# Token rows instead of feature rows for the values, gates and outputs of two recurrent phases

## The reference, cut to what matters

```python
# gated linear attention ("gla"): 4 heads, keys 128, values 256
S_t = diag(a_t) S_{t-1} + k_t^T v_t ;  o_t = q_t S_t      # a_t: forget gate
o_gla = rms_norm(o_gla, gla_out_norm) * silu(rg)          # norm over the 256 values of a head
# HGRN2 ("hg"): 16 heads, keys 128, values 128, the same recurrence with
# q = silu(.), forget = sigmoid(.), k = 1 - forget
o_hg = rms_norm_2(o_hg, hg_out_norm) * gate               # norm over the 128 values of a head
```

## Time and profile before

| | |
|---|---|
| median of 3 runs | 3389.58 us (3389.53 to 3390.03) |
| the profiled execution | 3386.4 us, its span 3384.6 us, granted clock 0.997 |
| PE matmul busy | 98% |
| DVE, ACT, POOL busy | 68%, 51%, 11% |
| DMA | 592 MB, 175 GB/s, queue 1 busy 56.1% |

### The profile page before, as it was taken

The page is one execution under the profiler, slowest core; times in us unless marked ns, Lnnn a source line. Parts: engine busy times, 40 slices in busy tenths (PEclk is TensorE's granted clock), DMA queues, the critical chain, the costliest instruction groups (busy, mean ns, idle before and its releaser), DMA issues.

```text
span 3384.6 us, 56343 instructions
## 1 busy us (share of the span) xinstructions
PE 3317.2 (98%) x18614; PEld 2866.3 (85%) x18614; DVE 2285.4 (68%) x3419; ACT 1714.9 (51%) x2500; POOL 379.8 (11%) x422
## 2 busy tenths in 40 slices
PE   8999999999999998999999999999999999999999
PEld 7888888887788877888888888888888888888888
DVE  6666666676656866665665677787666668656566
ACT  5444444454544655444444456774444444555554
POOL 1000000010022311000000001220242422100000
PEclk9999999999999999999999999999999999999999
DMA  7566566664544554666666655556544445555555
GB/s 227 186 199 187 185 192 186 188 190 144 160 147 148 193 155 138 187 190 187 187 191 187 185 181 176 189 178 188 162 149 149 149 149 164 184 162 180 169 168 166
DMA packets 236026, 592.48 MB, mean 175 GB/s; under 512 B 18832, under 2 KB 113296, under 8 KB 235808
## 3 DMA queue, kind: packets, MB, share of 16 engines
q1 hardware_dynamic: 234784, 587.12, 56.1%
q10 hardware_dynamic: 1152, 4.19, 0.3%
HBM read 589.14 MB, written 2.10 MB: 175 GB/s over the span
## 4 chain that ended last, share of the span: by engine, by line
PE 52%; issue 10%; DVE 3%; ACT 1%; POOL 1%; ACTq 0%; POOLq 0%
PE bank L495 31%; PE bank L494 8%; PE bank L497 8%; PE bank L733 2%; DVE w_low L1462 1%; PE bank L747 1%; POOL root_qk L2160 1%; ACT w_high L995 1%; DVE normed L1507 0%; PE bank L534 0%; PE bank L536 0%; PE bank L535 0%; DVE residual L1497 0%; PE bank L591 0%; PE bank L584 0%
## 5 line engine op out<-in xcount | busy, mean ns | idle before, releaser
L1462 DVE TENSOR_TENSOR w_low<-w_raw,w_high 128x1024 fp32r<-128x1024 f32 (+1 forms) x1120 | 1371.7, 1233 | 586.7 <-ACT w_high L995 567.8
L495 PE MATMUL bank<-normed,w_high 128*128 128x512 f32 x4800 | 1548.8, 399 | 14.6 <-DVE w_low L1462 10.3
L995 ACT ACTIVATE w_high<-w_raw 128x1024 fp32r<-128x1024 f32 (+1 forms) x1120 | 1165.8, 1044 | 696.0 <-PE bank L495 473.0
L495 PE MATMUL bank<-mixed,w_high 128*128 128x512 f32 x2496 | 794.2, 397 | 4.3 <-DVE increment L1494 4.3
L495 PEld LDWEIGHTS bank<-normed,w_high 128*128 128x128 f32 x4800 | 744.1, 189 | 17.9 <-issue 12.0
L494 PE MATMUL bank<-normed,w_low 128*128 128x256 f32 x2400 | 670.2, 279 | 0.0
L497 PE MATMUL bank<-normed,w_low 128*128 128x256 f32 x2400 | 667.3, 278 | 0.0
L494 PEld LDWEIGHTS bank<-normed,w_low 128*128 128x128 f32 x2400 | 451.9, 188 | 109.6
L497 PEld LDWEIGHTS bank<-normed,w_low 128*128 128x128 f32 x2400 | 453.1, 189 | 100.5 <-issue 1.7
L1012 ACT ACTIVATE parts<-bank 128x256 f32<-128x256 f32 x432 | 165.1, 382 | 689.3 <-PE bank L495 689.1
L495 PEld LDWEIGHTS bank<-mixed,w_high 128*128 128x128 f32 x2496 | 383.2, 189 | 7.0 <-issue 4.1
(11 more groups left out here) (288 smaller groups left out, 2367.5 us busy)
## 6 DMA issues: line engine op xcount, KB each, us to landing
w_raw<-w_hg SPq DMA_DIRECT2D x128, 512.0 KB, 3.6
w_raw<-w_att SPq DMA_DIRECT2D x128, 512.0 KB, 3.6
w_raw<-w_up1a SPq DMA_DIRECT2D x64, 512.0 KB, 4.2
w_raw<-w_up1b SPq DMA_DIRECT2D x64, 512.0 KB, 4.0
w_raw<-w_up2a SPq DMA_DIRECT2D x64, 512.0 KB, 4.2
w_raw<-w_up2b SPq DMA_DIRECT2D x64, 512.0 KB, 4.2
w_raw<-w_rg SPq DMA_DIRECT2D x64, 512.0 KB, 4.2
w_raw<-w_up1c SPq DMA_DIRECT2D x48, 512.0 KB, 4.0
```

The source lines that it names most:

```text
L495: last = nc.tensor.matmul(banks[b][:, :], hi, x, start=starts and k == 0, stop=stop)
L995: A_(wh[slot][:, 0:width], raw[slot][:, 0:width], ACT.Copy).then_inc(wh_done, 1)
L1462: TT(wl[slot][:, 0:width], raw[slot][:, 0:width], wh[slot][:, 0:width].bitcast(F32), ALU.subtract).then_inc(wl_done, 1)
```

## The change

In gla and hg the units of values and gates become token units. What is loaded changes accordingly: SP issues one DMA of four parts of 256 columns for a gla unit and two of half the size for an hg unit. Both accumulate in the banks `p_bc` and `p_o`; ACT evacuates them in slot 0 of the next body into values and silu of the gates. The transposes of V, the column sums, the diagonals and the spread go; the mix yields token rows, ACT squares it with a sum along the row, DVE scales a tiny variance, POOL takes the root, DVE multiplies rows, roots and gates in one operation for each block and head, PE turns the result with four transposes, and ACT and DVE write the high and low rows with the gain. All tables move, and the carried attention takes the mixer's normal order instead of `LAST_A`.

```diff
-        AT_G = {j: [(j + 2, 1)] for j in range(7)}
-        AT_G |= {7: [("mix", 1)], 8: [("norm", 1)], 9: [("diag", 1), ("prepare", 0)],
-                 11: [("spread", 1), ("values", 0), (0, 0), (1, 0)]}
-        AT_H = {j: [(j + 2, 1)] for j in range(7)}
-        AT_H |= {8: [("mix", 1)], 9: [("norm", 1)], 10: [("diag", 1)], 12: [("spread", 1), ("prepare", 0)],
-                 14: [("values", 0), (0, 0), (1, 0)]}
+        AT_G = {0: [("values", 1), (4, 1)], 1: [(5, 1)], 2: [(6, 1)], 3: [(7, 1)], 4: [(8, 1)], 6: [("mix", 1)],
+                7: [("norm", 1), ("prepare", 0)], 8: [("gate", 1)], 9: [(0, 0), (1, 0)], 10: [("oturn", 1), (2, 0)],
+                11: [("store", 1), (3, 0)]}
+        AT_H = {0: [("values", 1), (7, 1)], 1: [(8, 1)], 3: [("mix", 1)], 4: [("norm", 1)], 5: [("gate", 1)], 7: [("oturn", 1)],
+                8: [("prepare", 0)], 9: [("store", 1)], 10: [(0, 0), (1, 0)]}
+        AT_H |= {j: [(j - 9, 0)] for j in range(11, 16)}
...
-        LAST_A = AT_A | {2: [(("mix", 0), 1), (("weigh", 1), 1)], 3: [(("store", 0), 1), (("turn", 1), 1)], 4: [(("mix", 1), 1)],
-                         5: [(("store", 1), 1)], 6: [], 8: [], 9: []}
-        CARRIED = left(LAST_A, 2, 24)
+        CARRIED = left(AT_A, 2, 24)
...
+        FEATURES = {"gla": 4, "hg": 8, "rg": 8}
...
+                        for n, done in ((1, w_more), (0, w_in)):
+                            sp.dma_start(raw[slot][:, n * 4 * P:(n + 1) * 4 * P].rearrange("p (n c) -> p n c", c=2 * P),
+                                         src[i, 6 * n:6 * n + 2, m // 4, :, k0:k0 + 2 * P].rearrange("n p c -> p n c")
+                                         ).then_inc(done[slot], 16)
...
+                if step == "mix":
+                    pe.wait_ge(dec["placed"], it * 9 + 9)
+                    pe.wait_ge(rec["valued"], it + 1)
+                    for b, n, cols in head_columns(heads):
+                        to = p_sum[:, b * S:(b + 1) * S][:, cols]
+                        if b == 1:
+                            nc.tensor.matmul(to, ST[:, n, 1, :], V_D[:, 0, cols], start=True, stop=False)
+                        last = nc.tensor.matmul(to, ST[:, n, 2 * b, :], V_D[:, b, cols], start=b == 0, stop=True)
+                    last.then_inc(rec["mixed"], 1)
...
+                        if j < FEATURES[name]:
+                            unit2(qq, j, grp, XN, first and name in NORMED)
+                            continue
+                        m = j - FEATURES[name]
+                        if m == 0 and first and name == "gla":
+                            pe.wait_ge(att["maxed"], PAIRS)
+                        wait = (att["valued"], 2) if first and name == "gla" else (rec["valued"], i + it0)
+                        token_unit(name, qq, j, m, rec_banks, wait if m == 0 else None)
+                if step == "values":
+                    act.wait_ge(pe_unit, rec_end(it, heads))
+                    if not (isinstance(it, int) and it == 0):
+                        act.wait_ge(rec["gated"], it)
+                    for b in range(NB):
+                        A_(V_D[:, b, :], rec_banks[b][:, 0:S], ACT.Copy, scale=x_root[:, b:b + 1])
+                        last = A_(G_D[:, b, :], rec_banks[b][:, S:2 * S], ACT.Silu, scale=x_root[:, b:b + 1])
+                    last.then_inc(rec["valued"], 1)
+                if step == "norm":
+                    act.wait_ge(rec["mixed"], it + 1)
+                    for k, (b, n, cols) in enumerate(head_columns(heads)):
+                        last = A_(prod[:, b, cols], p_sum[:, b * S:(b + 1) * S][:, cols], ACT.Square,
+                                  accum_out=sum_rec[:, k:k + 1])
+                    last.then_inc(rec["squared"], 1)
...
+                if step == "gate":
+                    dve.wait_ge(rec["rooted"], it + 1)
+                    for k, (b, n, cols) in enumerate(head_columns(heads)):
+                        last = STT(out=O[:, b, cols], in0=p_sum[:, b * S:(b + 1) * S][:, cols], scalar=root_rec[:, k:k + 1],
+                                   in1=G_D[:, b, cols], op0=ALU.mult, op1=ALU.mult)
+                    last.then_inc(rec["gated"], 1)
+                if step == "store":
+                    dve.wait_ge(rec["high"], it + 1)
...
+                        last = STT(out=Y[:, rows, S:2 * S], in0=x[:, n0:n1, :], scalar=V_(gain, n0),
+                                   in1=Y[:, rows, 0:S].bitcast(F32), op0=ALU.mult, op1=ALU.subtract)
...
-                    dst = [V[:, 0, :], V[:, 1, :], *[A[:, n, :] for n in range(4)], G[:, 0, :], G[:, 1, :]]
+                    dst = [A[:, n, :] for n in range(4)]
```

More of the change, by code:

```diff
@@ L685, in gates, with decay @@
                     last.then_inc(gla["gate_sum"], 1)
[L687 to L699, removed]
+            def decay(step, it, heads):
+                if step == "mix":
[7 more added lines that the diff above has]
+                    last.then_inc(rec["mixed"], 1)
+                elif step == "oturn":
+                    pe.wait_ge(rec["gated"], it + 1)
                     for n in range(2):
@@ L702, in decay @@
                             last = nc.tensor.transpose(p_t[:, (2 * n + b) * P:(2 * n + b + 1) * P],
[L703 to L710, removed]
+                                                       O[:, b, n * P:(n + 1) * P], C_("ident"))
+                    last.then_inc(rec["turned"], 1)
                 elif isinstance(step, int):
                     b_out = (p_a, p_b)[step % 2]
+                    if step == 0:
+                        pe.wait_ge(dec["prepared"], it + 1)
                     if step == 1:
@@ L1062, in evacuates @@
                 return (j >= 2 and j < RING) if opens and j < RING else j % 2 == 1
[L1064 to L1076, removed]
             def attention(step, it, wide):
@@ new lines, in body @@
+                    mine = grp - takes[name]
+                    for j in range(nb):
+                        ahead(name, qq, j, nb, last)
+                        first = isinstance(i, int) and i == 0
+                        opens = first and name in NORMED
+                        if first:
+                            for step, h in opening.get(j, []):
+                                (opener or run)(step, h, 0)
+                        schedule(table, n, j, i, lambda s_, h: run(s_, h, mine + min(j, FEATURES[name]) // 2))
+                        if opens and j == 2:
+                            keep(name)
+                        if j < FEATURES[name] and evacuates(name, j, opens):
+                            k = j - 2 if opens and j < RING else j // 2
+                            part_out(qq, j, grp + k, k % 2)
@@ L1582, in diagonals @@
                 last.then_inc(h["diagonal"], 1)
-            def gate_step(it, heads, gain, y0):
-                dve.wait_ge(tail["spread"], it + 1)
-                for n in range(2):
-                    own.did(STT(out=O[:, n, :], in0=O[:, n, :], scalar=V_(gain, n if heads == 1 else 0),
-                                in1=p_bc[:, (n if heads == 2 else 0) * S:(n if heads == 2 else 0) * S + S],
-                                op0=ALU.mult, op1=ALU.mult))
-                own.settle()
-                dve.wait_ge(tail["silu"], it + 1)
-                both(O[:, :, :], GS[:, :, :], y0, tail["stored"])
             def both(a, b, y0, done):
@@ new lines, in body @@
+                    for j in range(nb):
+                        ahead(name, qq, j, nb, last)
+                        first = isinstance(i, int) and i == 0
+                        opens = first and name in NORMED
+                        if opens and j == 1:
+                            factors(name)
+                            TS(x_root[:, :], rstd[:, 0:NB], 1.0, None, ALU.mult)
+                        if opens and j == 2:
+                            dve.wait_ge(rms["kept"], NORMED[name] + 1)
+                        if first:
+                            for step, h in opening.get(j, []):
+                                (opener or run)(step, h)
+                        schedule(table, n, j, i, run)
+                        if j < FEATURES[name] and evacuates(name, j, opens):
+                            k = j - 2 if opens and j < RING else j // 2
+                            take(name, grp + k, k % 2, dst[k])
```

194 lines of the change are left out of this document (97 added, 97 removed).

## The result

The changed kernel took 3371.94 us (median of four runs, 3367.16 to 3372.93) beside 3389.81 us (3389.53 to 3390.15) of the kernel before on the same chip: ratio 0.9945, 95% interval 0.9931 to 0.9959. Faster by 17.9 us; forecast were 11.7. The profiled execution is the fastest of the four: 3367.16 us, span 3365.4 us.

A forecast was written before the change was run, and what follows sets the result against it. PE, busy 98% of the span, was taken as the bound. Gla 15.1 us faster less hg 3.4 us slower gave 11.7 off 3389.58, so 3378 us; own range 3370 to 3385, wider range 3364 to 3388.

The forecast's parts named there:

- Every wait named as going: In gla, PE's waits for DVE's score copies (4.4 us) and for the attention store (3.9 us) go.
- the one named as new: In gla's first head, the attention store in slot 9 ahead of DVE's first copies: 0.6 us once, bounds 0 and 1.5.
- preparing, before step 0: In hg, ACT's preparing takes 6.05 us against 5.44 of cover: PE loses 0.8 us an iteration with the restart.
- POOL's product, before step 1: In hg, POOL's 1.28 us after the preparing outlasts step 0's cover of 0.88: 0.4 us more an iteration.
- level 0 on POOL, before step 2: In hg, POOL's three operations have one unit of cover instead of two: 1.15 us an iteration, bounds 0.3 and 2.0.
- pace of the five rounds behind: In hg's levels 1 to 5, POOL sets the pace, swallowing 0.25 us of token gain plus 0.1 for step 3.
- The work that PE is freed of: In hg, per iteration: sums 0.89, spread 0.85 and eight token units at 0.067 make 2.28 us less PE work.
- The collision on POOL: In hg, a POOL operation meeting DVE's w_low stands until that ends: 1.60 us against 0.79 for the same operation.
- hg's waits would not arise: Rival: POOL and ACT finish inside the cover in hg, 21.6 us less, 3356 us; chance 0.06.
- gla's would only move: Rival: DVE's new store or the attention store holds gla's copies, so 4.4 + 3.9 us stay, 3386 us; chance 0.14.
- the chain on POOL would make it slower: Rival: hg's chain of levels costs PE over 2.3 us more an iteration than charged, for example 3397 us; chance 0.12.
- the token form gains nothing: Rival: gla loses 2.1 us of gain, hg almost nothing, 3380 us; inside the forecast's own range, no separate chance given.

The follow-up runs named there:

- the reordered kernel before: Kernel before, with gla's transposes and rounds 0 and 1 in slot 11 issued ahead of the old head's spread: 3385.01 us, ratio 0.9986.
- the squeezed variant: Changed kernel with the old squeezed order (LAST_A) for the attention heads carried into gla: 3373.68 us, ratio 0.9955.
- the sums put back: Changed kernel with the four one-column sums back on PE in each of 12 bodies, result unused: 3380.75 us, ratio 0.9976.
- the run with w_low cut: Changed kernel with DVE's w_low subtraction of hg's units cut from 1024 columns to 8: 3360.40 us, ratio 0.9919.
- the run with the gap: Changed kernel with hg's rounds 0 and 1 one slot later and rounds 2 to 8 two slots later, preparing unmoved: 3356.47 us, ratio 0.9904.

## Why the prediction was right, and where it missed

**The time** (3378 forecast, 3371.94 measured) lies inside the range and on the right side. Of the difference of 6.1 us, gla makes 2.9 and hg 3.8; the rest of the kernel gives back about half a microsecond.

**Gla.** Every wait named as going went, and the one named as new came (0.67 against 0.6 charged). The gate step as cause of round 2's waits is shown by the reordered kernel before, the squeezed order as cause of the long wait by the squeezed variant, the price of the sums by the sums put back (3.9 against 3.6). Taken from these runs, the three give 5.3 + 4.8 + 3.9 = 14.0 us, the new wait already taken off. The spread (1.7) and the token form (2.1), which I only argued and did not try alone, make it 17.8; measured 18.0. The terms that were mis-sized are both waits: 4.4 and 3.9 us, taken over as printed, were worth 5.3 and, with the slow matmuls behind, 5.5 (4.8 + 0.67). The granted clock of that stretch stood at 0.83 in the trace of before as well, and my sum had no term for it. It had none either for the mix, which in the kernel before stood 0.1 to 0.2 us late a head, as I read it behind step 8's copy; no run shows this alone. The sign that the prediction named for a gla head came out: 1.8 us shorter besides its wait was forecast. PE's rows give 40.68 us a head in the reordered kernel before (997.47 to 1038.15, from transposes to transposes) and 38.79 in the changed one (987.89 to 1026.68), 1.89 less.

**Hg.** The mechanisms were the ones charged; the prices were off by up to 0.3 us an iteration. An iteration (the first product on POOL to the next, mean of six) took 56.13 us before and 56.19 after; +0.42 was forecast. The waits in it, each as an interval between PE's rows less the same interval without the cause:

| term | charged | measured |
|---|---|---|
| preparing, before step 0 | 0.8 | 6.11 - 5.44 = 0.67 (slot 8 to round 0) |
| POOL's product, before step 1 | 0.4 | 1.35 - 0.89 = 0.46 |
| level 0 on POOL, before step 2 | 1.15 | 4.61 - 3.76 = 0.85 |
| pace of the five rounds behind | 0.35 | 0.10 + 0.17 + 0.11 + 0.06 + 0.13 = 0.57 |
| in all | 2.70 | 2.55 |

The intervals without the cause are those of the run with w_low cut, for the last two rows; their sum of 1.42 is just what that run's iteration is shorter by.

The term that was mis-sized most is level 0. In the kernel before POOL's three operations had taken 3.38 us, in the changed kernel they took 3.21, and the unit beside them, behind two rounds, covered 2.82 us (2425.07 to 2427.89) and not 2.72.

The pace row needs care: 0.35 was charged as a loss against the kernel before, while 0.57 is the loss against free rounds. In the kernel before POOL had already held four rounds (intervals of 3.82, 3.81, 3.80 and 3.88, from 2576.42 to 2591.73), by 0.55 us together against 3.67 and, for the last, an estimated 3.75. Set directly side by side, the five intervals were 18.98 us before and are 18.89 after, 0.09 less.

The work that PE is freed of was forecast as 2.28 us and comes out as 2.49 (56.19 - 2.55 = 53.64 against 56.13). Two corrections of opposite sign are in the rows: the 0.55 us of the held rounds, and less gain from the token form, since a token unit with a round takes 3.65 us, 0.02 less than 3.67 and not 0.067 less. Over six such units that is 0.28. With both, 2.28 becomes 2.55 (an estimate from these rows), near the 2.49.

**The collision on POOL**, which the prediction put against the change, is shown by the cut w_low: without it, POOL's product is back at 0.61 us and hg gets 11.4 us shorter. The Trainium skill, GPSIMD Engine Reference, section "1. Specifications", gives the rule that GpSimd contends with VectorE instructions that have two SBUF inputs; the trace agrees, with 0.61 us alone and 1.59 beside w_low. What the charge had wrong was its distribution: less at level 0, more at the levels without a printed wait.

**The rivals.** That hg's waits would not arise, that gla's would only move, and that the chain on POOL would make it slower are all contradicted by the waits of the changed kernel. That the token form gains nothing is contradicted by rows: ahead of round 0 in hg, 23 matmuls take 5.22 us (2416.69 to 2421.91), 0.227 each and 2.72 a unit, as in the earlier trace rows. In gla the 1.89 us a head make 7.6, less 3.9 for the sums and 1.7 for the spread; 2.0 us are left for the token form, with the mix in it. Next to a round it gains 0.02 us only.

**What the change left lying** is hg's table of slots. Its preparing stands two token units ahead of its first use and needs 6.1 us. One more slot and the free one behind round 1 are worth 15.0 us, nearly as much as the change itself, and the order of two POOL operations 4.4 more.

## What to carry to other kernels

A wait of PE can cost more than the profile prints: here some 0.3 us of restart each for the three waits of 1.48 us, and behind the one of 3.88 us matmuls ran at half clock for 3.1 us. So read the granted clock of the stretch behind a long wait before pricing it. Where work is taken off the bounding engine, the slots between a producer and its first use shrink with it: recompute each chain that hid there, and then move its start, as only a table had to change here. If small operations stand in a chain beside another engine's large ones, put those that nobody waits for last (worth 7.5 and 4.4 us here), and expect the collision to find the next operation.

## What was not expected of the hardware

- Rounds 4 to 7 of the recurrence stood 0.06 to 0.17 us further from the round before, without any wait printed for PE; only rounds set against a variant without the cause show it.
- The granted clock can also fall in cross attention, where waits of PE of 0.8 to 3.0 us follow one another. In windows of 10 us from 1150 to 1280, the second run of the changed kernel has these two, the others there are at 1.00:

```profile
1240.00:1250.00 10.00, 7.69 (x37) 6.03 (x35) 5.76 (x13) 9.16 (x21) 0.00 (x0) 0.94 0.29 79
1250.00:1260.00 10.00, 9.15 (x41) 7.35 (x40) 4.17 (x9) 3.72 (x7) 0.00 (x0) 0.89 0.42 135
```

  The kernel before showed 1.00 in all windows from 1150 to 1300, with waits of the same kind and lengths; the run with the gap showed 0.66 in one. The change touches nothing there. The time from the first w_mem load to the first w_up2a load was 116.1 us in the kernel before and between 117.3 and 120.6 in all other profiles. Differences of this size can blur totals. Nine runs of the kernel before lie between 3386.54 us, at a mean granted clock of 0.997, and 3391.47, at 0.995. That cross attention makes this spread is not shown: the two profiles of the changed kernel differ by 2.0 us in span but by 0.1 in cross attention, and 1.5 of it lies between the first w_up2a and the last w_rouA load. What decides in which runs the clock falls stays open.
